# A hybrid encoder layer: gate/up of the SwiGLU in Strassen's form, down as a stage of its own

## The reference, cut to what matters

```python
x  = x + concat(att, conv) @ w_out            # (2048, 1024) @ (1024, 1024)
z  = rms_norm(x, norm_ffn_g)
hid = silu(z @ w_gate) * (z @ w_up)           # (2048, 1024) @ (1024, 2816), twice
x  = x + hid @ w_down                         # (2048, 2816) @ (2816, 1024)
out = rms_norm(x, final_g)
```

## Time and profile before

| | |
|---|---|
| median of 3 runs | 3017.5 us (3016.28 to 3019.36) |
| span of the profiled execution, its own time | 3016.1 us, 34424 instructions |
| busy: PE, DVE, ACT, POOL | 95%, 50%, 29%, 17% |
| DMA | 170.74 MB, mean 57 GB/s |
| start of the part after the attention | 1272.7 us |

### The profile page before, as it was taken

How to read it: one execution, slowest core, us unless ns; L and a number is a source line. 1 busy time by engine, 2 the same in 40 slices (tenths; PEclk the granted TensorE clock), 3 DMA queues, 4 the chain that set the end, 5 groups by cost and what they waited for, 6 DMA issues and landing times.

```text
span 3016.1 us, 34424 instructions
## 1 busy us (share of the span) xinstructions
PE 2860.6 (95%) x12808; PEld 2289.8 (76%) x12808; DVE 1510.3 (50%) x2245; ACT 884.1 (29%) x1140; POOL 498.6 (17%) x263
## 2 busy tenths in 40 slices
PE   8999999889899999699999999999799999999997
PEld 6888888667777777587777777777577777777775
DVE  4100222589888888434444544444534444444445
ACT  5211000277676777422111111111321111111112
POOL 1000000177667677300000000000100000000001
PEclk9999999899999999799999999999899999999999
DMA  5322112111111200332111121110621111121101
GB/s 160 97 74 70 44 54 49 32 37 43 39 48 35 48 21 15 109 97 79 53 42 42 42 63 42 42 42 0 224 70 46 59 42 42 42 58 47 42 21 56
DMA packets 175320, 170.74 MB, mean 57 GB/s; under 512 B 9072, under 2 KB 140656, under 8 KB 174992
## 3 DMA queue, kind: packets, MB, share of 16 engines
q1 hardware_dynamic: 172368, 160.40, 17.9%
q10 hardware_dynamic: 2880, 9.44, 0.8%
HBM read 139.40 MB, written 30.41 MB: 56 GB/s over the span
## 4 chain that ended last, share of the span: by engine, by line
issue 64%; PE 29%; DVE 3%; POOL 2%; ACT 2%; DVEq 0%; DMA 0%; ACTq 0%; SPq 0%; POOLq 0%
PE projected L1159 17%; PE scores L1217 4%; PE o_sum L1242 4%; PE tile_turned L1235 2%; DVE a_t_lo L976 1%; POOL exp L524 1%; POOL row_rstd L542 1%; ACT exp L663 1%; ACT a_t_hi L673 1%; PE u_turned L1168 0%; PE o_norm L1279 0%; POOL exp L521 0%; DVE row_max L961 0%; DVE exp L961 0%; PE projected L1151 0%
## 5 line engine op out<-in xcount | busy, mean ns | idle before, releaser
L1328 PE MATMUL gate_up<-z_t_hi,gate_up_part_hi 128*128 128x512 f32 x1408 | 560.8, 398 | 10.6 <-DVE gate_up_part_lo L1071 10.6
L1328 PE MATMUL gate_up<-z_t_lo,gate_up_part_hi 128*128 128x512 f32 x1408 | 560.5, 398 | 0.0
L1328 PE MATMUL gate_up<-z_t_hi,gate_up_part_lo 128*128 128x512 f32 x1408 | 560.1, 398 | 0.0
L1051 DVE TENSOR_TENSOR rows<-y_sum,rows 128x1024 f32<-128x1024 f32 x368 | 450.2, 1223 | 92.2 <-PE y_sum L1308 68.1
L1082 DVE TENSOR_TENSOR hid<-gate_up,gate_silu 128x512 f32<-128x512 f32 x88 | 60.9, 692 | 742.8 <-ACT gate_silu L774 742.8
L774 ACT ACTIVATE gate_silu<-gate_up 128x512 f32<-128x512 f32 x88 | 52.5, 597 | 1012.6 <-PE gate_up L1328 1012.6
L961 DVE CUSTOM_DVE_ANT_0 exp<-scores,window 128x1024 f32<-128x1024 f32 x256 | 310.2, 1220 | 35.1 <-issue 34.8
L1328 PEld LDWEIGHTS gate_up<-z_t_hi,gate_up_part_hi 128*128 128x128 f32 x1408 | 266.6, 189 | 75.1 <-issue 11.1
L1328 PEld LDWEIGHTS gate_up<-z_t_hi,gate_up_part_lo 128*128 128x128 f32 x1408 | 266.6, 189 | 64.5
L1328 PEld LDWEIGHTS gate_up<-z_t_lo,gate_up_part_hi 128*128 128x128 f32 x1408 | 266.6, 189 | 63.7
L542 POOL TENSOR_TENSOR row_rstd<-row_mean,neg_half 128x1 f32<-128x1 f32 x32 | 24.9, 783 | 1730.2 <-DVE row_mean L1055 1730.2
(11 more groups left out here) (122 smaller groups left out, 3735.0 us busy)
## 6 DMA issues: line engine op xcount, KB each, us to landing
gate_up_raw<-in_w_gate SPq DMA_DIRECT2D x44, 512.0 KB, 4.0
gate_up_raw<-in_w_up SPq DMA_DIRECT2D x44, 512.0 KB, 5.3
down_raw<-in_w_down SPq DMA_DIRECT2D x44, 512.0 KB, 5.9
w_raw<-in_w_in SPq DMA_DIRECT2D x24, 512.0 KB, 5.1
projected_t<-stage SPq DMA_DIRECT2D x48, 256.0 KB, 2.4
x_tile<-in_x SPq DMA_DIRECT2D x16, 512.0 KB, 4.3
q_stage<-projected_t SPq DMA_DIRECT2D x32, 256.0 KB, 4.7
o_raw<-in_w_out SPq DMA_DIRECT2D x16, 512.0 KB, 8.4
```

The lines of the kernel that those rows point to most:

```text
L1051: nc.vector.tensor_tensor(rows[:, i], y_sum[:, slot], rows[:, i], ALU.add).then_inc(y_added, 1)
L1328: last = nc.tensor.matmul(gate_up[:, b, g], gu_part[w][:, slot, g, kt], z_t[z][:, kt, b * BANK:(b + 1) * BANK], start=(kt == 0 and n == 0) ...
```

## The change

The halves' loop is gone; there are three stages over all 2048 rows.

*Projection.* Sixteen tiles n in the order of ORDER (tiles of the two blocks of a half in turn), with `m_raw` and `rows` in two buffers each. The rows are stored to DRAM after the residual. The transposed z of a pair of tiles is copied to SBUF (`zt`), GpSimd makes four sums and differences of its k halves and blocks (`sum_z`), and seven pieces of 128 x (4 x 128) go to DRAM (`store_z`).

*Gate/up.* A step is one chunk of one half, 44 in all. With a11, a12 the k halves of w_gate, a21, a22 those of w_up, b11, b21 the k halves of z of block 0 and b12, b22 those of block 1, the eight block products become seven (Winograd's variant of Strassen's form): s1 = a21 + a22, s2 = s1 - a11, s3 = a11 - a21, s4 = a12 - s2; t1 = b12 - b11, t2 = b22 - t1, t3 = b22 - b12, t4 = b21 - t2. The products, in order 0 to 6: a11 b11, s2 t2, a12 b21, s3 t3, s1 t1, a22 t4, s4 b22, each 12 matmuls 128x512. Products 0 and 2 share a bank, also 3 and 5, and 4 and 6: the second adds onto the first. VectorE makes u2 = P0 + P1, u3 = u2 + P3, up 1 = u3 + P4, up 0 = u2 + (P3 + P5), gate 1 = u2 + (P4 + P6). GpSimd makes s1 to s4 for each step from the one raw buffer of the weights (`sum_weights`). The seven parts of z for a half lie in `z_slot`; those of the first half are loaded at the end of the projection, those of the second during step 21. hid goes to DRAM (`store_hid`).

*Down.* Four groups of 512 rows, each over 22 chunks; hid and w_down's rows are loaded for each chunk, split again, and the sums of four tiles stay in all eight banks of PSUM over the 22 chunks. Then VectorE adds the rows, loaded from DRAM, and norms; the stores go by GpSimd's queue.

```diff
+        z_slot = [[at(SLOT * k + 8192 * n, f"z_{'hi' if n == 0 else 'lo'}_{k}", [P, 4, BANK], F32R) for n in range(2)] for k in range(7)]
+        o_part = [at(3 * SLOT + 32768 * n, f"o_part_{'hi' if n == 0 else 'lo'}", [P, KT, D], F32R) for n in range(2)]
+        o_raw = at(0, "o_raw", [P, KT, D])
...
+        w_slot = [[at(tail + 4096 * k + 2048 * n, f"w_{'hi' if n == 0 else 'lo'}_{k}", [P, 4, P], F32R) for n in range(2)] for k in range(7)]
...
+        gu_raw = at(tail + 61440, "gate_up_raw", [P, 2, KT, P])
...
+        BANK_OF = (0, 1, 0, 2, 3, 2, 3)
...
+            def load_m(n):
+                if n >= 2:
+                    sp.wait_ge(m_lo_ready, n - 1)
+                i = ORDER[n]
...
-                    sp.dma_start(m_raw[:, i % 4, part], src.rearrange("(kt p) s -> p kt s", p=P)[:, :, bass.ds(half * HALF + i * P, P)]
...
+                    sp.dma_start(m_raw[:, n % 2, part], src.rearrange("(kt p) s -> p kt s", p=P)[:, :, i * P:(i + 1) * P]
+                                 ).then_inc(m_loaded[n % 2], 16)
...
+            def load_rows(n):
+                i = ORDER[n]
+                if n >= 2:
+                    sp.wait_ge(rows_stored[n % 2], 16 * (n // 2))
+                    sp.wait_ge(z_ready, n - 1)
+                sp.dma_start(rows[:, n % 2], x_rows[i * P:(i + 1) * P, :]).then_inc(rows_loaded[n % 2], 16)
+            def store_rows(n):
+                i = ORDER[n]
+                sp.wait_ge(rows_added, n + 1)
+                sp.dma_start(rows_dram[i * P:(i + 1) * P, :], rows[:, n % 2]).then_inc(rows_stored[n % 2], 16)
...
+            def store_z(pair):
+                half, column = pair // 4, pair % 4 * P
+                sp.wait_ge(zt_ready, 2 * pair + 2)
+                for k, src in ((0, zt[:, 0, 0:4]), (2, zt[:, 0, 4:8]), (6, zt[:, 1, 4:8])):
+                    sp.dma_start(z_dram[half, k, :, :, column:column + P].rearrange("k p t -> p k t"), src).then_inc(z_stored[half], 16)
+                for n, k in ((0, 4), (1, 1), (2, 3), (3, 5)):
+                    sp.wait_ge(zt_sum_ready, 4 * pair + n + 1)
+                    sp.dma_start(z_dram[half, k, :, :, column:column + P].rearrange("k p t -> p k t"), zt_sum[:, n]).then_inc(z_stored[half], 16)
...
+            def load_gate_up(step, chunk):
+                sp.wait_ge(w_lo_ready_2, 7 * step)
...
-                    load_rows(half, i - 1)
-                load_rows(half, TILES - 1)
-                sp.wait_ge(m_lo_ready, 4 + TILES * half + TILES)
-                sp.sem_inc(load_due, 1)
-                load_chunk(half, 0, 0)
...
...
+            def store_hid(half, step, chunk, b):
+                sp.wait_ge(hid_ready, 2 + 2 * step + b + 1)
+                sp.dma_start(hid_dram[bass.ds(chunk, 1), :, half * HALF + b * BANK:half * HALF + (b + 1) * BANK].rearrange("o p t -> p (o t)"),
+                             hid_stage[:, b]).then_inc(hid_stored[b], 16)
...
+            def load_z_late(k):
...
+                sp.wait_ge(z_lo_ready, k - 1)
+                if k == 4:
+                    sp.wait_ge(z_ready, N_ROWS)
+                    sp.wait_ge(rows_stored[0], 16 * (N_ROWS // 2))
+                    sp.wait_ge(rows_stored[1], 16 * (N_ROWS // 2))
+                sp.dma_start(z_stage[(k + 1) % 2][:, :, :], z_dram[0, k].rearrange("k p t -> p k t")).then_inc(z_loaded[(k + 1) % 2], 16)
...
+            load_z_late(4)
+            store_z(N_ROWS // 2 - 1)
+            load_z_late(5)
+            load_z_late(6)
+            load_gate_up(1, 1)
+            store_hid(0, 0, 0, 0)
+            store_hid(0, 0, 0, 1)
+            with sp.Fori(1, F_CHUNKS - 1) as chunk:
+                load_gate_up(chunk + 1, chunk + 1)
+                store_hid(0, chunk, chunk, 0)
+                store_hid(0, chunk, chunk, 1)
+            load_z_next(0)
+            load_z_next(1)
+            load_gate_up(F_CHUNKS, 0)
+            for k in range(2, 5):
+                load_z_next(k)
+            store_hid(0, F_CHUNKS - 1, F_CHUNKS - 1, 0)
+            load_z_next(5)
+            load_z_next(6)
+            store_hid(0, F_CHUNKS - 1, F_CHUNKS - 1, 1)
+            with sp.Fori(0, F_CHUNKS - 1) as chunk:
+                load_gate_up(chunk + F_CHUNKS + 1, chunk + 1)
+                store_hid(1, chunk + F_CHUNKS, chunk, 0)
+                store_hid(1, chunk + F_CHUNKS, chunk, 1)
...
+            def load_down(group, chunk, slot, wait=True):
+                if wait:
+                    sp.wait_ge(f_lo_ready, 2 * (F_CHUNKS * group + chunk) - 2)
+                sp.dma_start(hid_raw[:, slot], hid_dram[bass.ds(chunk, 1), :, group * BANK:(group + 1) * BANK].rearrange("o p t -> p (o t)")
+                             ).then_inc(hid_loaded[slot], 16)
+                sp.dma_start(down_raw[:, slot], w_down[0, bass.ds(chunk * P, P), :]).then_inc(down_loaded[slot], 16)
...
+            def sum_weights(step):
+                pool.wait_ge(gu_loaded, 32 * step + 32)
+                a11, a12, a21, a22 = gu_raw[:, 0, 0:4], gu_raw[:, 0, 4:8], gu_raw[:, 1, 0:4], gu_raw[:, 1, 4:8]
+                s1, s2, s3, s4 = (w_sum[:, n] for n in range(4))
+                nc.gpsimd.tensor_tensor(s1, a21, a22, ALU.add).then_inc(w_sum_ready, 1)
+                pool.wait_ge(w_sum_ready, 4 * step + 1)
+                nc.gpsimd.tensor_tensor(s2, s1, a11, ALU.subtract).then_inc(w_sum_ready, 1)
+                nc.gpsimd.tensor_tensor(s3, a11, a21, ALU.subtract).then_inc(w_sum_ready, 1)
+                pool.wait_ge(w_sum_ready, 4 * step + 2)
+                nc.gpsimd.tensor_tensor(s4, a12, s2, ALU.subtract).then_inc(w_sum_ready, 1)
...
+            def split_w(step, k, first=False):
+                if not first:
+                    act.wait_ge(product_ready, 7 * step - 7 + k + 1)
+                src, n_sum = ((gu_raw[:, 0, 0:4], 0), (w_sum[:, 1], 2), (gu_raw[:, 0, 4:8], 0), (w_sum[:, 2], 3), (w_sum[:, 0], 1),
+                              (gu_raw[:, 1, 4:8], 0), (w_sum[:, 3], 4))[k]
+                act.wait_ge(gu_loaded, 32 * step + 32)
+                if n_sum:
+                    act.wait_ge(w_sum_ready, 4 * step + n_sum)
+                nc.scalar.activation(w_slot[k][0][:, :, :], src, ACT.Copy).then_inc(w_hi_ready_2, 1)
...
+            def gate_up_step(step, later=None):
+                copy_p_0(step)
+                for k in range(7):
+                    if k == 2:
+                        silu_first(step)
+                    split_w(step + 1, k)
+                    if later:
+                        later(k)
+                silu_second(step)
...
+            def split_w(step, k):
+                src = (gu_raw[:, 0, 0:4], w_sum[:, 1], gu_raw[:, 0, 4:8], w_sum[:, 2], w_sum[:, 0], gu_raw[:, 1, 4:8], w_sum[:, 3])[k]
+                dve.wait_ge(w_hi_ready_2, 7 * step + k + 1)
+                nc.vector.tensor_tensor(w_slot[k][1][:, :, :], src, w_slot[k][0][:, :, :].bitcast(FP32), ALU.subtract).then_inc(w_lo_ready_2, 1)
+            def combine(step, out_tile, product, bank, addend, after):
+                dve.wait_ge(product_ready, 7 * step + product + 1)
+                dve.wait_ge(combined, 5 * step + after + 5)
+                nc.vector.tensor_tensor(out_tile[:, :], c_bank[bank], addend[:, :], ALU.add).then_inc(combined, 1)
+            def make_u_2(step):
+                dve.wait_ge(hid_ready, 2 + 2 * step)
+                dve.wait_ge(p_0_ready, step + 1)
+                combine(step, u_2, 1, 1, p_0, 0)
...
+            def make_u_3(step):
+                combine(step, u_3, 3, 2, u_2, U2)
...
+            def hidden(step, b):
+                if b == 0:
+                    dve.wait_ge(silu_0_ready, step + 1)
+                    dve.wait_ge(combined, 5 * step + C21 + 5)
+                else:
+                    dve.wait_ge(silu_1_ready, step + 1)
+                dve.wait_ge(hid_stored[b], 16 * step + 16)
...
+            def gate_up_step(step, later=None, split=True):
+                for k in range(7):
+                    if k == 1:
+                        make_u_2(step)
+                    if k == 3:
+                        make_u_3(step)
+                    if k == 4:
+                        make_c_22(step)
+                    if k == 5:
+                        make_c_21(step)
+                        hidden(step, 0)
+                    if k == 6:
+                        make_c_12(step)
+                    if split:
+                        split_w(step + 1, k)
+                    if later:
+                        later(k)
+                hidden(step, 1)
...
+            def block_product(step, k, fresh=None):
+                pe.wait_ge(w_lo_ready_2, 7 * step + k + 1)
+                if fresh is not None:
+                    pe.wait_ge(z_lo_ready, 7 * fresh + k + 1)
+                if k == 0:
+                    pe.wait_ge(silu_0_ready, step)
+                if k == 1:
+                    pe.wait_ge(combined, 5 * step - 5 + U2 + 5)
+                if k == 2:
+                    pe.wait_ge(p_0_ready, step + 1)
```

(95 more changed lines are left out.)

671 lines of the change are left out of this document (372 added, 299 removed).

## The result

The kernel after takes 3121.9 us (median of 4 runs, 3117.3 to 3125.1), the kernel before 3016.9 beside it (4 runs). The ratio is 1.0345, 95% interval 1.0331 to 1.036. The forecast was 3051 us: the direction is right and 3121.9 lies in the range of 2985 to 3130, but outside the main case's own 3025 to 3100. That range reached to 3130 for rivals 3 and 4, which did not occur, and left rival 2's mechanism out; that the time lies in it is luck. The change costs 105 us where 34 were forecast. The profiled execution has a span of 3118.0 us.

A forecast was written before the change was run, and what follows sets the result against it. TensorE's matmuls were taken to bound the kernel. Up to the projection 1272.7, projection 246.4, gate/up 865, waits 88, 30 and 37, down 4 and 488, end 18.7 sum to 3049.8, median 3051 us; range 2985 to 3130.

The forecast's parts named there:

- the main case: Whole kernel: fewer matmuls, but new waits cost more; 3051 us, own range 3025 to 3100, chance 0.51.
- rivals 3 and 4: 3: down starves on late loads, 3090 to 3140 us, 0.04; 4: matmuls each stretch 0.01 us, 3090 us, 0.03.
- rival 2: Gate/up steps: a wait near 3.5 us drops the clock, 3.1 us a step, 40 times, 3175 us; chance 0.10.
- The matmuls saved: Gate/up: 84 matmuls for a chunk and half in place of 96, 0.234 us each, 124 us less.
- The wait in each step: Gate/up: product 5 waits for make_u_3 behind weight load, sums and splits; 2.2 us a step, at most 3.3.
- 2.2 us a step, in 40 steps 88 us: Gate/up: the wait before product 5 over 40 steps, added to the forecast as 88 us.
- The projection: Projection to first product: one SP queue's loads and stores delay TensorE, 47 us over seven pairs; 246.4 us in all.
- First step and turn: Waits in gate/up's first step, 30 us (20 to 40), and at the half's turn, step 21, 37 us (20 to 50).
- Down: Down stage: loads hidden, no idle, 2112 matmuls at 0.231 us, 488 us; 4 us for its first split.
- Rival 1: Gate/up: VectorE and GpSimd don't exclude each other or loads land sooner; wait 0 to 0.8 us, about 2990 us; chance 0.25.

The follow-up runs named there:

- e2_warm: Kernel after with ten more matmuls ahead of product 5's wait for make_u_3, in every step but the first; 3054.7 us, ratio to before 1.012.
- e9_warm3: Kernel after with three more matmuls ahead of product 5's wait for make_u_3; 3124.3 us, ratio to before 1.0354.
- e6_proj: Kernel after with the load of projection tile n+3 issued in round n, ahead of the stores, in place of tile n+2's; 3082.4 us, ratio to before 1.0219.
- e5_nosum: Kernel after without GpSimd's sums of weights, the splits reading raw blocks (only its time is of use); 2916.0 us, ratio to before 0.9665.
- e1_order: Kernel after with VectorE's order in a gate/up step changed, make_u_3 behind the first weight split, not the third; 2914.4 us, ratio to before 0.9651.

## Why the forecast was wrong, step by step

- **The matmuls saved**: right. They are 0.227 to 0.231 apart where nothing is waited for, slightly less than the 0.234 taken, in down 0.228 in place of 0.231 (480.93 us for 2112). That is worth 7 us in down. In gate/up it is worth next to nothing in the kernel after: there the chain sets the step, and faster matmuls ahead of product 5 only lengthen the wait.
- **The wait in each step**: the mechanism is right, link by link. The size is 0.6 us too small: product 5 starts 16.9 us after product 0 on average, not 16.25, in 37 steps 24 of the 71 us missing. All of it is the load: the first sum starts at 9.8, not 9.0, 0.3 of this by a later issue and the rest by a later landing, while the chain behind it is 0.2 shorter than forecast. That chain was priced with 1.25 us for sums 1 and 3 and 1.15 for 2 and 4, with 0.69 for the first split and 0.55 for the other two, without a word on the difference; with 1.25 and 0.69 throughout it would have come to 16.8. The order of time bears the lower prices out (1.15 and 1.12, 0.54 to 0.56). The Trainium skill's rule (GPSIMD Engine Reference, Elementwise — side-by-side cycle accounting), 1.11 us for such an operation as an estimate, lies below the 1.29; the line drawn through the two rows of before, 1.30, was the better price.
- **"2.2 us a step, in 40 steps 88 us"**: this is the step that failed. It prices the wait as the time in which TensorE stands still and nothing more. The wait also takes the clock down behind itself, 1.6 us each time, 59 us in 37 steps (e2_warm). The forecast knew this as rival 2, gave it 0.10, tied it to a wait near 3.5 because the row of before showed a fall after 5.3, and priced it at 3.1 us. It came at waits of 2.7 to 3.8 in every steady step, and with e9_warm3 from 2.0 on, and cost half as much: some 3 us at 1.2 GHz, not 15 matmuls. So neither the main case nor rival 2 is what happened, but the first's wait with the second's mechanism. Among the forecast's rows there was none between no idle and 5.3 us of it, and the condition was set inside that gap without a reason. The trace of before has such rows, in the attention. Idles of 2.3, 2.5 and 2.5 us end at 621.6, 819.6 and 987.2, and each time the granted clock is 0.50 less than a microsecond later, though an idle of 1.9 us that ends at 862.3 left it at full. The first of them, and the window behind it:

```profile
621.62 0.63 PE L1235 MATMUL tile_turned<-identity,v_stage 128*128 128x128 f32 x4 [2.31 <-DVE a_t_lo L976]
622.40:625.80 3.40, 3.40 (x11) 0.50 0.02 5
```

- **The projection**: 237.8 against 246.4, cause as forecast (e6_proj). **First step and turn**: 1.8 and 3.8 us over. **Down**: no wait past its first two chunks, as forecast; rivals 3 and 4 did not occur.
- **Rival 1**: its mechanism (no exclusion between such short operations) is wrong by e5_nosum; but its time comes, and more, from another order on VectorE (e1_order, 2914.4 us).

Worked out again with the two corrections, 0.6 and 1.6 in 37 steps: 3051 + 81 is 3132; less the 8.7 of the projection and the 8.6 of down it is 3115, against 3121.9 measured; the first step, the turn and the distance of the median to the span hold the rest.
